# Hybrid decoder layer: output projection and MLP with features on the partitions, the second norm's factor moved to the final sums

## What is computed

```python
merged = gates[:, :, 0] * y_attn + gates[:, :, 1] * y_pool
x = x + einsum('bsd,de->bse', merged, w_o)
h2 = rms_norm(x, norm2_g)            # x * rsqrt(mean(x*x) + 1e-6) * g, per token
u = square(relu(einsum('bsd,df->bsf', h2, w_mlp_in)))   # 4096 hidden features
x = x + einsum('bsf,fd->bsd', u, w_mlp_out)
```

## Time and profile before

| | us |
|---|---|
| median of 3 runs | 1242.21 (1241.85 to 1242.36) |
| the profiled execution | 1241.36 |
| its span, first to last instruction | 1239.5 |
| PE busy | 1228.6 |
| DVE busy | 945.4 |
| ACT busy | 563.9 |
| POOL busy | 139.2 |

### The profile page before, as it was taken

How to read it: one execution, slowest core, us unless ns; L and a number is a source line. 1 busy time by engine, 2 the same in 40 slices (tenths; PEclk the granted TensorE clock), 3 DMA queues, 4 the chain that set the end, 5 groups by cost and what they waited for, 6 DMA issues and landing times.

```text
span 1239.5 us, 16100 instructions
## 1 busy us (share of the span) xinstructions
PE 1228.6 (99%) x5822; PEld 1014.1 (82%) x5822; DVE 945.4 (76%) x1334; ACT 563.9 (45%) x971; POOL 139.2 (11%) x188
## 2 busy tenths in 40 slices
PE   8999999999999999999999999999999999999999
PEld 6878888887878888888888888888888888888887
DVE  6857876788887597845678867777769988879764
ACT  7546666665644323312345544535545333333330
POOL 1122233224100040000000000000000000000035
PEclk9999999999999999999999999999999999999999
DMA  9201211023564556422214354353479544262223
GB/s 368 78 17 35 64 40 35 19 60 95 175 235 159 184 172 221 169 86 85 102 60 162 133 173 161 129 178 139 150 263 367 210 157 152 100 237 102 102 100 138
DMA packets 111662, 173.95 MB, mean 140 GB/s; under 512 B 6240, under 2 KB 56288, under 8 KB 111584
## 3 DMA queue, kind: packets, MB, share of 16 engines
q1 hardware_dynamic: 111440, 172.92, 39.9%
q10 hardware_dynamic: 144, 0.00, 0.0%
HBM read 122.57 MB, written 50.33 MB: 139 GB/s over the span
## 4 chain that ended last, share of the span: by engine, by line
PE 88%; DVE 6%; ACT 3%; issue 2%; DMA 1%; SPq 0%; POOL 0%; ACTq 0%; DVEq 0%; POOLq 0%
PE bank L2337 79%; PE bank L2512 2%; PE bank L2467 2%; PE bank L2446 2%; PE bank L2404 1%; DMA x_tile<-in_x 1%; DVE c L2237 1%; DVE pair_lo L2131 1%; PE bank L2395 1%; DVE slot_lo L1532 1%; PE bank L2661 1%; DVE small L1622 1%; ACT prob L1102 0%; DVE gate_w_f L1882 0%; ACT slot_hi L1037 0%
## 5 line engine op out<-in xcount | busy, mean ns | idle before, releaser
L2337 PE MATMUL bank<-o_hi,s_lo 128*128 128x512 f32 (+1 forms) x452 | 175.0, 387 | 0.0
L2337 PE MATMUL bank<-o_hi,s_hi 128*128 128x512 f32 (+1 forms) x452 | 175.0, 387 | 0.0
L2237 DVE TENSOR_TENSOR c<-bank,c 128x512 f32<-128x512 f32 x112 | 75.7, 689 | 34.5 <-PE bank L2337 32.9
L2337 PE MATMUL bank<-featT_hi,pair_hi 128*128 128x512 f32 x256 | 99.8, 390 | 0.8 <-DVE c L2237 0.8
L2337 PE MATMUL bank<-o_lo,s_hi 128*128 128x512 f32 (+1 forms) x260 | 100.3, 386 | 0.0
L2337 PE MATMUL bank<-featT_lo,pair_hi 128*128 128x512 f32 x256 | 99.6, 389 | 0.0
L2337 PE MATMUL bank<-featT_hi,pair_lo 128*128 128x512 f32 x256 | 99.6, 389 | 0.0
L2337 PEld LDWEIGHTS bank<-o_hi,s_lo 128*128 128x128 f32 x452 | 84.9, 188 | 17.3
L2337 PEld LDWEIGHTS bank<-o_hi,s_hi 128*128 128x128 f32 x452 | 84.9, 188 | 17.2
L1500 ACT ACTIVATE s_hi<-s_raw 128x2048 fp32r<-128x2048 f32 x28 | 53.7, 1917 | 95.5 <-DMA s_raw<-u_store 95.5
L1476 ACT ACTIVATE c<-c 128x512 f32<-128x512 f32 x64 | 40.0, 625 | 118.9 <-DVE c L2237 118.9
(11 more groups left out here) (270 smaller groups left out, 3135.8 us busy)
## 6 DMA issues: line engine op xcount, KB each, us to landing
s_raw<-u_store SPq DMA_DIRECT2D x28, 1024.0 KB, 5.6
pair_raw<-in_w_mlp_in SPq DMA_DIRECT2D x16, 1024.0 KB, 5.7
u_store<-s_tile SPq DMA_DIRECT2D x64, 256.0 KB, 2.1
o_raw<-in_w_mlp_out SPq DMA_DIRECT2D x16, 1024.0 KB, 8.0
u_store<-u_tile SPq DMA_DIRECT2D x48, 256.0 KB, 2.3
gate_store<-out_tile SPq DMA_DIRECT2D x32, 256.0 KB, 2.1
gate_raw<-in_w_in SPq DMA_DIRECT2D x8, 1024.0 KB, 5.3
front<-in_v_and_high SPq DMA_DIRECT2D x8, 512.0 KB, 7.8
```

The costliest lines, as they stand in the source:

```text
L2237: nc.vector.tensor_tensor(out[:], psum, other[:], ALU.add).then_inc(up_sum, 1)
L2337: mm = nc.tensor.matmul(out, a, b, start=start and i == 0, stop=stop and i == len(steps) - 1, skip_group_check=onto)
```

## The change

The output projection gives feature tiles: weights are stationary, 512 tokens move; `out_projection(n)` makes one of eight feature tiles for one half of the tokens, the upper half first. x is read from the arrays `v_and_high` and `x_low`, which hold it turned. The transposes are gone. The norm's g is applied by ACT when it copies a sum to `z` (`gain`), and the operands of the MLP are made of z, those of the upper half while the projection of the lower half runs. The factor of each token, 1/sqrt(m) with m = mean(x*x) + 1e-6, is left out: relu and square of unnormed operands come out m times too large. The sum over the features of a token is a matmul of the squares (split in two) with a matrix of ones (`token_squares`), for the upper half in the projection, for the lower half ahead of pair 2; `token_mean` makes m of it. In pairs 4 to 11 the pieces of the residual are fetched, multiplied by m and stored again (`load_plain`, `scale_res`, `store_scaled`). In pairs 12 and 13 DVE takes the reciprocal of m (`mean_inverse`). In the second half of the MLP weights are stationary and u moves; the finished sums are multiplied by 1/m (`out_scale`, 16 pieces), for the last product its u operand instead (`scale_last_s`). The result is written turned, and the host turns it back. Pair order is plain: all of pair 0, then pair 1. Four places hold raw pair weights, the first two only for pairs 0 and 1.

```diff
-            def h2_transpose(s):
-                ...
-                for b in range(2):
-                    for k in range(4):
-                        mm = nc.tensor.transpose(bank[:, h2_bank(s, b), k * P:(k + 1) * P],
-                                                 h2_row[:, kk * P:(kk + 1) * P], ident[:])
+            def out_projection(n):
+                d, half = out_tile_of(n), out_half(n)
+                ...
+                    mm = passes(bank[:, n % 4, :], [(cut(w, ALL, k % 2, slice(d % 4 * P, (d % 4 + 1) * P)),
+                                                     cut(featT, ALL, k, HALVES[half]))], start=k == 0, stop=k == KD - 1)
+            def token_squares(half):
+                ...
+                for i, part in enumerate((square_hi, square_lo)):
+                    mm = nc.tensor.matmul(bank[:, SQUARES_BANK[half], :], square_ones[:], part[half][:], start=i == 0, stop=i == 1)
+            for n in range(OUTS):
+                if n == KD + 4:
+                    token_squares(1)
+                out_projection(n)
-            product(0, P5)
-            product(0, P4)
-            product(1, P5)
-            h2_transpose(T - 1)
-            product(1, P4)
             for p in range(PAIRS):
-                for i in range(0 if p > 1 else 2, 7):
+                if p == 2:
+                    token_squares(0)
+                for i in range(7):
                     product(p, i)
...
-                           [(cut(left, ALL, k, cols), cut(right, ALL, k)) for k in range(4)]).then_inc(d_tile, 1)
+                           [(cut(right, ALL, k, cols), cut(left, ALL, k)) for k in range(4)]).then_inc(d_tile, 1)
```

SP in the seam, and in the pairs:

```diff
+            for n in range(OUTS):
+                store_res(n)
+                if 0 < n < OUTS - 2:
+                    if n % KD == 1:
+                        sp.wait_ge(squared, n)
+                    else:
+                        sp.wait_ge(square_added, square_count(n - 1))
+                    load_res(n + 2)
+                if n == OUTS - 4:
+                    sp.wait_ge(side_sum2, SIDE_SUM["s2", 1])
+                    load_pair(0)
+                if n == OUTS - 2:
+                    sp.wait_ge(side_sum2, SIDE_SUM["s2", 3])
                     load_pair(1)
...
                     load_pair(p + 2)
+                if 1 <= p - 2 <= KD:
+                    load_plain(p - 2)
...
                 store_u(D1, p, u_tile[0])
+                if 1 <= p - 3 <= KD:
+                    store_scaled(p - 3)
```

DVE in the seam, in the pairs and at the end:

```diff
+            for k in range(4):
+                t_sum(0, k)
+            add_res(OUTS - 2)
             t_split_lo(0, P5)
             t_split_lo(0, P4)
+            difference_sums(QK - 1)
+            side_part_lo("s4", QK - 2)
+            t_split_lo(0, P1)
+            top_lo(0)
+            square_add(OUTS - 3)
+            add_res(OUTS - 1)
+            t_split_lo(0, P6)
+            fourth_sum(QK - 1)
+            side_part_lo("s2", QK - 1)
+            t_split_lo(0, P2)
+            top_lo(1)
+            token_mean(1)
+            side_part_lo("s3", QK - 1)
+            t_split_lo(0, P7)
+            side_part_lo("s4", QK - 1)
+            t_split_lo(0, P3)
+            square_add(OUTS - 2)
+            square_add(OUTS - 1)
...
+                if 1 <= p - 3 <= KD:
+                    scale_res(p - 3, 0)
+                    scale_res(p - 3, 1)
+                elif p - 3 > KD and p - KD - 4 < 2:
+                    mean_inverse(p - KD - 4)
                 dve.wait_ge(p_done, turn(p, P7))
                 up_add(4, c22, p7, c21)
...
+                nc.vector.reciprocal(mean[half][:], mean[half][:]).then_inc(inverse_ready, 1)
...
+                if n == DOWN - 5:
+                    for t in range(QN):
+                        out_scale(t, 0, d_added, 4 * (DOWN - 7) + t + 1)
...
-            for i in range(len(LAST_PARTS)):
+            for t in range(QN):
+                out_scale(QN + t, 1, folded, 3 * QN + t + 1)
+                if t % 2 == 1:
+                    last_add(t // 2)
+            for i in range(2, len(LAST_PARTS)):
                 last_add(i)
```

More of the change, by code:

```diff
@@ L1411, in _, with gain @@
             merged_hi(KD - 1, LOW, KD + 1)
[L1413 to L1433, removed]
-                    for i, (pair, src) in enumerate(((comb2, s2_f), (comb3, s34_f), (comb4, s34_f))):
-                        act.wait_ge(h2_f, f + 1 + i)
-                        copy_hi(pair[0][:, :, cols], src[:])
+            def gain(n):
+                d = out_tile_of(n)
+                z = (z_low, z_high)[out_half(n)]
+                act.wait_ge(res_ready, n + 1)
+                nc.scalar.activation(z[:, d % QK, d // QK], res[n % 3][:], ACT.Copy,
+                                     scale=col[:, G2 + d:G2 + d + 1]).then_inc(z_ready, 1)
@@ new lines, in top_hi @@
+            def top_hi(second):
+                for i in range(2):
+                    two = slice(2 * i, 2 * i + 2)
+                    act.wait_ge(z_ready, OUTS - 1 + second)
+                    if second:
+                        act.wait_ge(wo_full, OUTS)
+                    else:
+                        act.wait_ge(wo_left, 5)
+                    nc.scalar.activation(featT[0][:, QK * second + 2 * i:QK * second + 2 * i + 2, LOW], z_low[:, two, second],
+                                         ACT.Copy).then_inc(side_hi2, 1)
@@ L1504, in _ @@
                 if more:
-                    for i in range(2 if p == 0 else 0, 5):
+                    for i in range(2 if p == 0 else 5):
                         t_split_hi(p + 1, i)
@@ L2198, in _ @@
-            t_sum(0, 2)
-            add_res(T - 1, 0)
-            t_sum(0, 3)
+            for n in range(KD):
+                add_res(n)
+                if n % 2 == 1:
+                    bottom_sum(n // 2)
+                elif n > 0:
+                    bottom_lo(n // 2 - 1)
+                if n > 1:
+                    square_add(n - 1)
+            for n in range(KD, OUTS - 2):
+                j, second = divmod(n - KD, 2)
+                add_res(n)
+                if second:
+                    fourth_sum(j)
+                    if j == 0:
+                        square_low_part(1)
+                    side_part_lo("s3", j)
+                    side_part_lo("s2", j)
+                else:
+                    difference_sums(j)
+                    if j == 0:
+                        bottom_lo(QK - 1)
+                    else:
+                        side_part_lo("s4", j - 1)
+                if n != KD + 1:
+                    square_add(n - 1)
```

510 lines of the change are left out of this document (292 added, 218 removed).

## The result

The changed kernel takes **1244.13 us** (median) against 1242.21: a ratio of 1.0020, 95% interval 1.0012 to 1.0027 (the medians alone give 1.0015). By the medians that is 1.9 us slower, where 3.3 us faster was forecast, and above the range of 1236.0 to 1242.8. The profiled execution took 1244.11 us with a span of 1242.3 us.

The account below looks back on a forecast made before the run. PE (TensorE) was taken as the bound, busy 1228.6 of 1239.5 us. Terms -7.0 + 0.9 - 1.3 + 1.9 + 2.2 = -3.3 gave 1238.1 us profiled, 1238.9 us median; range 1236.0 to 1242.8.

Parts of the forecast that it names:

- The tail: End of the MLP: DVE's added multiplies by 1/m fit beside GpSimd's sums and the last add isn't delayed; 0.
- 25 x 0.6 = 15 us: Last two products, 21.9 us: DVE's twelve multiplies and 13 adds, each priced at 0.6 us.
- more of y still in flight: Kernel's end: worst case for result pieces not yet stored, at most 0.7 us.
- The seam: From projection to MLP: PE waits for DVE before P4 of pairs 1 and 2; +1.9 us (0.5 to 4.6).
- The reciprocals: Pairs 12 and 13: two DVE reciprocals outlast the time available and make PE wait; +2.2 us, bounds 0 and 5.6.
- R: Time of one 128x512 DVE reciprocal, taken as 3.0 us.
- cover: In a steady pair, how much later up_add 4 may start on DVE without PE waiting: 1.89 us.
- What leaves PE: The 64 transposes go, eight sets of eight at 0.875 us each; -7.0 us.
- What comes to PE: Two token_squares of two 128x512 matmuls each, +0.9 us; all other matmuls unchanged in number and width.
- a term of its own (-1.3): Two existing PE stalls at the start of the MLP, before P4 of a pair, taken out; -1.3 us.
- The rivals: One-pass reciprocal (1236.7 us, chance 0.20), eightfold reciprocal (1241.7 us, 0.25), DVE starving between projection and MLP (1246.4 us, 0.10).
- a starved seam: Rival between projection and MLP: bare ACT handovers make DVE and PE 7.5 us later; 1246.4 us, chance 0.10.

Follow-up runs that it names:

- after: The changed kernel as it was, without further edit, and its profile: median 1244.13 us, ratio 1.0020 to the kernel before.
- t1: Changed kernel with GpSimd's eight last sums cut from 512 to 8 columns, the rest left out: 1240.33 us.
- t3: Changed kernel with the last twelve multiplies by the norm's factor cut from 512 to 8 columns: 1239.60 us.
- t4: Changed kernel, no work left out, ScalarE copying the factor into PSUM, where the last twelve multiplies read it: 1240.33 us.
- t1 to t4: Four one-edit versions of the changed kernel: t1, t3, t4, and one storing the lower rows of y's last tiles in halves (1241.79 us).
- x1: Kernel before the change with four of the eight transposes of each token tile left out: 1239.66 us, ratio 0.9979.

## Why the prediction was wrong

**What fell: "The tail", priced at 0.** The step "25 x 0.6 = 15 us" used' spacing for multiplies that run beside GpSimd. The text took the earlier trace rows' 3.37 as a price that GpSimd alone pays, and its limit of 0.7 for "more of y still in flight" supposed that DVE was in time. The rows there show both sides: DVE's 2048-column operation took 2.85 in the earlier trace rows, where the same size takes 2.28 at 1195.13 in the changed kernel, before GpSimd's first sum there at 1198.09; so DVE paid as well. GpSimd was even early: its last sum was forecast for 1233.7 and ended at 1230.13. Worked out from after's rows: GpSimd's sums, when nothing disturbs, follow by 1.25 (1213.11 to 1214.36). Four multiplies with three sums taken in between would be 4 x 0.60 + 3 x 1.25 = 6.15; from the first of the four to the next operation are 6.03. Six with one sum would be 4.85; measured so, 4.83. One by one, multiplies start at 1220.69, 1222.39 and 1224.08 and sums at 1220.15, 1221.88 and 1223.57: one of each every 1.70. The engines take turns, an instruction at a time.

That is +4.8 on DVE, and the last two products (from 1212.9 on) had no room for it. The prediction had found 15 us of work there for 21.9, but the last low part and a wait for PE fell into them too:

```profile
1213.71 2.84 DVE L2301 TENSOR_TENSOR s_lo<-s_raw,s_hi 128x2048 fp32r<-128x2048 f32 x1
...
1218.54 0.69 DVE L2434 TENSOR_TENSOR acc<-acc,bank 128x512 f32<-128x512 f32 x1 [0.80 <-PE bank L2513]
```

So 21.9 - 15 - 2.8 - 0.8 = 3.3 were to spare, and 4.8 is 1.5 too much; the last add came 1.3 later against the last matmul.

t1 (GpSimd's work removed), t3 (DVE's removed) and t4 (one operand moved) each bring the end back to 3.0 to 3.4.

The Trainium skill (SBUF — State Buffer, "Who interferes with whom") states this: a VectorE instruction with two SBUF inputs contends with a GpSimd instruction that reads SBUF, and the pair of ports that they share is an exclusive lock. The rows of t1 and t4 agree (2.50 for four multiplies without the sums, 1.88 for three with one operand in PSUM). The prediction drew on no such rule; the rule spoke against the change.

**"The seam", +1.9: right, with one margin too thin.** The load was to let DVE start at -6.0; t1's starts at -5.97. P4 of pair 1 was to be 1.4 late; by PE's starts it is 1.5 late in t1 to t4. P4 of pair 2 was to be 0.4 late; it is 0.35 to 0.38. The slow restart adds 0.08 each time, and up to 0.2 goes in front of P2 of pair 0: together about 2.1. P2 was to be met with 0.1 to spare. That was too thin: in after's execution, where the load came 0.9 later, PE waited 0.74 there, its start came 0.9 late, and the seam cost 3.0.

**"The reciprocals", +2.2: mis-sized by 0.6.** R is 3.35, not 3.0. For each, PE's start comes 1.32 late (idle 1.16 by the record) and the restart takes 0.08, some 1.4 in all: 2.8. Its place, its cover and its waits came as worked out. From 256 to 512 columns it is (3348 - 1746) / 256 = 6.26 ns a column, six times the slope of 1.04. The repeat count of eight that the Trainium skill gives (VectorE: DVE Perf Modes, "First, the fixed hardware budget"), taken as eight times that slope, is not borne out. The two-element row had pointed at 5.5 ns a column, over a distance of 510 columns.

**"What leaves PE" and "What comes to PE": right.** The projection is 5.91 shorter, 5.7 forecast. The set in the seam was entered at 0.875 like the others. x1's smaller saving there does not speak against that: 0.19 of it went into a wait of which the sum has a term of its own (-1.3).

**Right at 0:** no wait in pairs 4 to 11; `scale_res` takes 1.29 of the cover of 1.89, and the pieces' transfers show in no wait of PE.

**The sum again**, from the typical profiles t1 to t4: -5.9 in the projection, 614.8 - 611.6 = +3.2 in the MLP (forecast +2.4), so -2.7 up to the last matmul. Of the 0.8 by which the MLP misses, the reciprocals are 0.6 and the seam 0.2. With the end's 4.7 it is 2.0 slower; 1.9 was measured by the medians. The rivals had nothing of this: the chance for slower lay on a starved seam, and the place that decided had been closed with one engine's price.

## What to carry to other kernels

When work is moved onto an engine beside another that shares a path with it, price both: where long rows of the two meet, each engine pays for the other's instructions, and the sum of both must fit, not each alone. At the end of a kernel nothing hides lateness: ask when each piece of the result becomes ready, and how many bytes are then still to go. A multiplier that is reused can be put in PSUM once, so that the elementwise work no longer needs two SBUF operands; by itself it turned some 2 us slower into some 2 us faster here.

## What was not expected of the hardware

- Elementwise instructions of DVE (two SBUF operands) and GpSimd (SBUF) take turns whole: four multiplies followed by 1.5 on average instead of 0.60, and by 1.70 where each met a sum. Six sums of GpSimd took 10.95 instead of 6 x 1.25 = 7.5; of the difference, 2.1 is the first sum, which took 3.34 beside DVE's 2048-column low part, and the rest lies beside the multiplies.
- With the DMA engines at 352 GB/s (share 0.92), SP's issues of y's last four pieces took 0.65 to 1.2 us each, back to back (3.91 for four).
- A DVE reciprocal costs 6.26 ns a column plus some 0.14 us: 164 ns for 2, 1746 for 256, 3348 for 512.
